# A two-layer decoder step on one core: another order in the routing with filler products, another order of the first layer's loads, and v in other PSUM banks

## The chip, the core and the metric

The kernel runs on one NeuronCore of a Trainium2 chip. The metric is the time of one execution on the device, in microseconds (us), as the median of several runs. The engines are TensorE (PE, with its weight loads shown as PEld), VectorE (DVE), ScalarE (ACT), GpSimd (POOL) and SyncE (SP), which issues nearly all transfers.

## What is computed

A decoder trunk of two layers over 288 tokens (32 of running sequences, 256 of a new one), 1024 features, all in float32:

```python
h = rmsnorm(x); z = h @ w_in                       # 1024 -> ua | ub | v, 512 each
# group A: diagonal complex state space model, 32 groups of 16 channels, 64 states
h_t = ab * h_(t-1) + bb @ ua_t ; ya = glu(gelu(Re(c @ h_t) + d * ua_t))
# group B: gated unit, 8 heads of 64, chunks of 128 positions
v = layernorm(gelu(v)) ; yb = gelu(ub) * (tril(w_s) @ v + b_s)
x = x + [rmsnorm(ya), rmsnorm(yb)] @ w_out
x = x + ffn(rmsnorm(x))     # layer 0: dense SwiGLU; layer 1: top 2 of 8 experts
```

Outputs are the final rmsnorm of x, the last states of both kinds of sequences, and the normalised v of the 32 running tokens.

## The kernel before

Every engine has one program, written out by hand in the order in which it works; they meet by semaphores (`wait_ge`, `then_inc`), and each engine takes its instructions strictly in order. Features lie on the 128 partitions, tokens on the free axis (KT = 8 blocks of x), so a 288-column product per weight block is the usual one. A float32 product shows as two records in the trace, each with a weight load. The expert and dense phases split each weight into a high part (ACT) and a low part (DVE, POOL) and use three products.

*Start and mixer (each layer).* SP loads cols, x, consts, misc, then `load_in`: B (`b_d`, lines 527 to 528, straight into the slots of BPX, in pieces of 32 numbers), w_in in four pieces (0 and 1 are the halves of ua's columns by feature block, 2 is v's, 3 is ub's), C, and small tables. PE waits for the constants (line 1035), sums the squares of x (`mean_sum`), forms ua with `u_half` in banks 0 to 3, then v in banks 0 to 2 (lines 1063 to 1068), then transposes the powers of B, four for each of n = 0 to 7, into banks n % 4 (lines 1071 to 1081), then the states' inputs (s, L1090), ub in banks 4 to 7 (L1098), the gates of the spatial unit (L1119 to L1128, four of them, ft = 0 to 3), with the kernel matrices K (L1112) ahead of ft = 2, then y (L1141, L1147), the GLU, and w_out (L1196, L1205).

ACT forms the roots, copies ua into `ust` (16 copies, L855), applies GELU to the three token tiles of v (`gelu_v`, L821), takes the deviations (`deviation`, L826), centres tiles 1 and 2 of v by eight instructions of 64 columns each (`centre`, L833), copies the transposed B (BT, L868) and s (L877), applies GELU to ub (L882), copies K (L886). In layer 0 ACT's first functions are exp and sin for the angles.

DVE (the helper at line 1412 holds every tensor_tensor) forms the angles, h of layer 0 by `gained`, the powers of B (BPX), scales ua, takes the statistics of v (`statistics`), forms the carried states (`carried`), normalises v (`layer_norm`), then does the states in two halves (rotate, scan L1654 and L1655, rotate back, `st_ready`), with the scaling of ub (`gate_rows`) between. layer_norm(2) stands behind the first scan, 0 and 1 before the states.

POOL forms the rotations (L663 to L678, layer 0 here, layer 1 in the dense phase), masks the spatial weights (L694), then the powers of C (CPX, L701 to L711, `cp_ready`), the diagonal, and adds it to K (L725, `k_ready`). PE waits for `cp_ready` at L1112 and for `k_ready` before y. SP loads w_out when the states are ready (`st_ready`, line 562), in the order of the feature blocks; its first half overlays B's powers and the state inputs.

*Routing (behind layer 1's w_out).* PE finishes transposes of the tokens (banks by `tok_bank`) and logits (`lg_mm`); DVE forms the two best experts of each token, `mask`, and the low parts of the tokens (L1785, six), PE the positions in each expert and the totals (L1269, L1271), DVE the one-hot tables (`one_hots`, L1795); ACT the high parts of the tokens (L945). PE gathers the tokens of two experts (`gather`, four times ten products of 256 columns, L1282 to L1285), ACT and DVE split them, and the first expert's gate products follow (L1294). SP waits for the number of passes (`ni_ready`) before it loads further expert weights.

## Time and profile before

| | us |
|---|---|
| median of 3 runs | 976.8 |
| lowest and highest | 972.62 and 979.61 |
| the profiled execution | 980.57 |
| its span, first to last instruction | 978.8 |
| mean granted clock of TensorE | 0.970 of full |

PE is busy for 930.1 us of the span, DVE for 713.5, ACT for 522.3, POOL for 321.7. An engine that is busy less than the span waits for others in the rest; only the engine that the end hangs on counts, and here PE is on 81% of the chain that ended last. A granted clock of 1.00 is 2.4 GHz, 0.50 is 1.2 GHz.

### The profile page before, as it was taken

The numbers are of one execution on the slowest core, as the hardware profiler recorded it, in microseconds if no ns is written. First come the engines' busy times: TensorE is split into PE (matmuls) and PEld (weight loads), VectorE is DVE, ScalarE is ACT, GpSimd is POOL, SyncE is SP. The second block draws the span as 40 slices with busy tenths as digits, with TensorE's granted clock in tenths as the row PEclk, the third lists the DMA queues.
The fourth block names the chain that finished last, engine by engine and source line by source line (L and its number), as shares of the span: only waits on it lengthen the run. The fifth ranks groups of instructions, "written<-read, shape, count | busy, mean of one in ns | idle before, by whom it ended". The sixth has DMA issues, their size and how long they took to land.

```text
span 978.8 us, 15158 instructions
## 1 busy us (share of the span) xinstructions
PE 930.1 (95%) x5526; PEld 789.7 (81%) x5526; DVE 713.5 (73%) x1032; ACT 522.3 (53%) x679; POOL 321.7 (33%) x260
## 2 busy tenths in 40 slices
PE   6999999998999999799998999999999999999895
PEld 4486779998999996386787888878888888878774
DVE  7799557574355508976375497988799988898784
ACT  3661445553333402661542567776777867685762
POOL 6996002212348100960020042231514051414220
PEclk9998999998999999987998999999999999999998
DMA  9500835554554118201800689897998989898861
GB/s 277 163 1 4 307 87 189 167 165 132 151 162 152 59 44 226 104 4 63 348 1 30 232 290 361 288 384 273 328 311 326 339 299 334 290 379 271 363 210 49
DMA packets 95564, 199.65 MB, mean 204 GB/s; under 512 B 34194, under 2 KB 55922, under 8 KB 95508
## 3 DMA queue, kind: packets, MB, share of 16 engines
q1 hardware_dynamic: 94708, 197.88, 59.1%
q8 instruction: 36, 0.59, 0.2%
q10 hardware_dynamic: 576, 0.59, 0.2%
q0 software_dynamic: 224, 0.43, 0.1%
q14 instruction: 20, 0.16, 0.0%
HBM read 197.27 MB, written 1.61 MB: 203 GB/s over the span
## 4 chain that ended last, share of the span: by engine, by line
PE 81%; DVE 10%; DMA 3%; issue 3%; ACT 2%; SPq 1%; DVEq 0%; ACTq 0%
PE ps L1295 8%; PE ps L1294 8%; PE ps L1297 8%; PE ps L1031 7%; PE ps L1032 7%; PE ps L1033 6%; PE ps L1205 5%; PE ps L1365 4%; PE ps L1366 4%; PE ps L1369 4%; PE ps L1044 2%; DVE M L1412 2%; PE ps L1098 2%; PE ps L1196 2%; PE ps L1026 1%
## 5 line engine op out<-in xcount | busy, mean ns | idle before, releaser
L1412 DVE TENSOR_TENSOR wrnd_u<-wraw_u,wrnd_u 128x1376 fp32r<-128x1376 f32 (+1 forms) x80 | 144.7, 1839 | 5.6 <-ACT wrnd_u L784 5.5
L784 ACT ACTIVATE wrnd_g<-wraw_g 128x1376 fp32r<-128x1376 f32 (+2 forms) x96 | 115.1, 1212 | 59.6 <-DMA wraw_g<-in_moe_w_down 36.5
L648 POOL TENSOR_TENSOR wrnd_g<-wraw_g,wrnd_g 128x1024 fp32r<-128x1024 f32 (+2 forms) x16 | 47.6, 2973 | 258.9 <-ACT wrnd_g L784 258.9
L1412 DVE TENSOR_TENSOR wrnd_g<-wraw_g,wrnd_g 128x1376 fp32r<-128x1376 f32 (+1 forms) x80 | 119.6, 1506 | 15.6 <-ACT wrnd_g L784 15.5
L784 ACT ACTIVATE wrnd_u<-wraw_u 128x1376 fp32r<-128x1376 f32 (+1 forms) x96 | 115.7, 1256 | 11.1 <-DMA wraw_u<-in_moe_w_gate 7.0
L648 POOL TENSOR_TENSOR wrnd_u<-wraw_u,wrnd_u 128x1376 fp32r<-128x1376 f32 (+1 forms) x16 | 52.4, 3275 | 80.8 <-ACT wrnd_u L784 80.8
L1031 PE MATMUL ps<-Md,split_u 128*128 128x288 f32 (+2 forms) x240 | 71.7, 299 | 5.4 <-DVE rs L1412 5.4
L1412 DVE TENSOR_TENSOR xb<-xb,ps 128x288 f32<-128x288 f32 x96 | 39.5, 445 | 50.2 <-PE ps L1205 25.6
L1033 PE MATMUL ps<-Md,split_u 128*128 128x288 f32 (+2 forms) x240 | 70.9, 296 | 0.0
L1031 PE MATMUL ps<-Md,split_d 128*128 128x288 f32 (+2 forms) x224 | 66.6, 297 | 0.8 <-DVE xb L1412 0.8
L1033 PE MATMUL ps<-Md,split_d 128*128 128x288 f32 (+2 forms) x224 | 66.2, 295 | 0.0
L1031 PEld LDWEIGHTS ps<-Md,split_u 128*128 128x128 f32 (+2 forms) x240 | 45.1, 188 | 5.9 <-DVE rs L1412 5.9
L1205 PE MATMUL ps<-D 128*128 128x288 f32 x192 | 49.3, 409 | 0.0
L1412 DVE TENSOR_TENSOR split_u<-raw,split_u 128x1024 fp32r<-128x1024 f32 (+2 forms) x22 | 29.3, 1332 | 27.3 <-ACT split_u L778 27.3
L1412 DVE TENSOR_TENSOR split_d<-raw,split_d 128x1024 fp32r<-128x1024 f32 (+2 forms) x21 | 29.7, 1424 | 26.5 <-ACT split_d L778 26.4
L640 POOL TENSOR_TENSOR split_u<-raw,split_u 128x1024 fp32r<-128x1024 f32 x8 | 19.9, 2482 | 82.6 <-ACT split_u L778 82.6
L640 POOL TENSOR_TENSOR split_d<-raw,split_d 128x1024 fp32r<-128x1024 f32 x7 | 17.1, 2444 | 89.1 <-ACT split_d L778 89.1
L1033 PEld LDWEIGHTS ps<-Md,split_u 128*128 128x128 f32 (+2 forms) x240 | 45.2, 189 | 0.0
L1032 PE MATMUL ps<-hbr,split_d 128*128 128x288 f32 (+1 forms) x152 | 45.2, 297 | 0.0
L1032 PE MATMUL ps<-hbr,split_u 128*128 128x288 f32 (+1 forms) x152 | 45.1, 297 | 0.0
L1205 PEld LDWEIGHTS ps<-D 128*128 128x128 f32 x192 | 36.0, 190 | 9.4
L1031 PEld LDWEIGHTS ps<-Md,split_d 128*128 128x128 f32 (+2 forms) x224 | 42.5, 190 | 1.0 <-DVE xb L1412 1.0
(355 smaller groups left out, 2662.0 us busy)
## 6 DMA issues: line engine op xcount, KB each, us to landing
wraw_u<-in_moe_w_gate SPq DMA_DIRECT2D x39, 688.0 KB, 6.5
wraw_g<-in_moe_w_up SPq DMA_DIRECT2D x32, 688.0 KB, 7.2
wraw_g<-in_moe_w_down SPq DMA_DIRECT2D x39, 512.0 KB, 4.5
wraw_u<-in_moe_w_down SPq DMA_DIRECT2D x33, 512.0 KB, 4.4
wraw_u<-in_moe_w_up SPq DMA_DIRECT2D x24, 688.0 KB, 6.1
wraw_g<-in_moe_w_gate SPq DMA_DIRECT2D x18, 688.0 KB, 5.7
raw<-in_ffn_w_gate SPq DMA_DIRECT2D x20, 512.0 KB, 4.5
raw<-in_ffn_w_up SPq DMA_DIRECT2D x20, 512.0 KB, 4.0
```

The costliest lines, as they stand in the source:

```text
L648: pool.tensor_tensor(lo[0:r, 0:w], raw_half(n)[0:r, 0:w], hi[0:r, 0:w].bitcast(F32), ALU.subtract).then_inc(w_lo_pool, 1)
L784: act.activation(halves(n)[0][0:r, 0:w], raw_half(n)[0:r, 0:w], ACT.Copy).then_inc(w_hi, 1)
L1031: pe.matmul(out, w_hi, x_hi, start=start, stop=False)
L1032: pe.matmul(out, w_hi, x_lo, start=False, stop=False)
L1033: return pe.matmul(out, w_lo, x_hi, start=False, stop=stop)
L1205: mm = pe.matmul(bank(out_bank[m]), w_out[:, k, m * P:(m + 1) * P], yn(k), start=(m >= 4 and k == 0), stop=(k == (MT - 1 if m < 4 else KT ...
L1294: pe.matmul(o, hg_h[hg][:, k, :], w_hi[:, f0:f1], start=(k == 0), stop=False)
L1295: pe.matmul(o, hg_h[hg][:, k, :], w_lo[:, f0:f1], start=False, stop=False)
L1297: mm = pe.matmul(ps[:, b0 + b, 0:f1 - f0], hg_l[hg][:, k, :], w_hi[:, f0:f1], start=False, stop=(k == KT - 1))
L1365: pe.matmul(ps[:, 6 + z, :], het_h[0:r, k, :], w_hi[0:r, f], start=(k == 0), stop=False)
L1366: pe.matmul(ps[:, 6 + z, :], het_h[0:r, k, :], w_lo[0:r, f], start=False, stop=False)
L1412: return dve.tensor_tensor(o, a, b, op)
```

## The change

- Routing: ACT and DVE take the token blocks in the order in which the gather reads them (TOK_ORDER), DVE forms three low parts before the one-hot tables and three behind; the first gather uses the banks 3, 5, 4, 6; the totals of the experts are formed between the second and third gather; 11 and 6 products of `ones` by `ones` into bank 0 stand ahead of the waits for the mask and for the tokens. The early `exp` on ACT that only loaded its table is gone. The first `lead_low` stands ahead of the gates' arithmetic.
- First layer: `ones` is written by DVE and not loaded; PE begins with 18 products of it; consts and misc are loaded behind w_in's second piece; B is loaded as one transfer with rows of 4 KB into a buffer of its own (`b_raw`, which overlays POOL's ct1 and ct2, so POOL waits for `b_used`); h of layer 0 is formed by ACT behind the squares.
- v goes to banks 4 to 6, so v doesn't wait for ua's banks, and the transposes of B wait for ua alone; the states' inputs wait for all of v's GELUs. One deviation for all three tiles stands behind the copies of BT; ACT centres all three tiles, 24 instructions, behind the copies of the states' inputs; DVE does all three layer norms behind its first scan.
- w_out: the second half is loaded as soon as all state inputs are multiplied, the first when the states are ready.

```diff
+TOK_ORDER = (2, 4, 0, 3, 5, 1)
+LEAD_BANK = (3, 5, 4, 6)
+FILL_MASK, FILL_TOK = 11, 6
...
+WARM_START = 18
...
+        b_raw = D[:, 5248:6272].rearrange("p (r n f) -> p r n f", r=2, n=NP)
...
-            sp.dma_start(consts[:, :], consts_d).then_inc(const_in, 16)
-            sp.dma_start(misc[:, :], misc_d).then_inc(const_in, 16)
...
-                for r in range(2):
-                    sp.dma_start(BPX[:, r, :, 0, :], b_d[l, :, r]).then_inc(prep_in, 16)
+                else:
+                    piece(0, 0, 4, 0)
+                sp.dma_start(b_raw, b_d[l]).then_inc(prep_in, 16)
+                piece(1, 4, KT, 0)
                 if l == 0:
-                    piece(0, 0, 4, 0)
-                piece(1, 4, KT, 0)
+                    sp.dma_start(consts[:, 0:4 * P], consts_d[:, 0:4 * P]).then_inc(const_in, 16)
+                    sp.dma_start(misc[:, :], misc_d).then_inc(const_in, 16)
...
-                for j in range(PIECES):
+                for j in (2, 3, 0, 1):
+                    if j == 0:
+                        sp.wait_ge(st_ready, 2 * (l + 1))
                     sp.dma_start(w_out[:, 2 * j:2 * j + 2, :], src[:, 2 * j:2 * j + 2, :]).then_inc(w_out_in[j], 16)
...
-                sp.wait_ge(st_ready, 2 * (l + 1))
+                sp.wait_ge(s_mm, 4 * (l + 1))
...
+                pool.wait_ge(b_used, l + 1)
...
-                    act.activation(v[0:n, t, :], ps[0:n, t, :], ACT.Gelu_apprx_tanh,
+                    act.activation(v[0:n, t, :], ps[0:n, 4 + t, :], ACT.Gelu_apprx_tanh,
                                    scale=r_tok[0:n, t:t + 1]).then_inc(v_ready, 1)
...
-                def deviation(g0, g1, n):
-                    act.wait_ge(var_ready, 2 * l + n)
-                    act.activation(std[:, g0:g1], stat[:, g0:g1, 1], ACT.Sqrt,
-                                   bias=eps[:, 0:1]).then_inc(std_ready, 1)
...
                 def centre(t):
-                    act.wait_ge(nmr_ready, 2 * l + t)
+                    n = TILES[t][1]
+                    act.wait_ge(nmr_ready, l + 1)
...
+                    for k in range(KT):
+                        act.activation(h[:, k, :], x[:, k, :], ACT.Copy, scale=col(0, "norm_mix", k)).then_inc(h_ready, 1)
...
-                deviation(0, 16, 1)
-                centre(1)
...
-                deviation(16, 24, 2)
+                act.wait_ge(var_ready, l + 1)
+                act.activation(std, stat[:, :, 1], ACT.Sqrt, bias=eps[:, 0:1]).then_inc(std_ready, 1)
...
-                centre(2)
+                for t in range(3):
+                    centre(t)
...
-            act.activation(warm, eps[:, 0:1], ACT.Exp)
...
-            for n in range(6):
+            for n in TOK_ORDER:
...
-            pe.wait_ge(const_in, 32)
+            pe.wait_ge(ones_ready, 1)
+            for n in range(WARM_START):
+                pe.matmul(bank(6, P), ones, ones, start=True, stop=True)
...
-                    pe.wait_ge(ua_ready, 4 * l + t + 1)
...
-                        mm = pe.matmul(ps[0:n, t, :], h[:, k, t0:t0 + n], w_in[:, k, 2 * MIX:IN_W],
+                        mm = pe.matmul(ps[0:n, 4 + t, :], h[:, k, t0:t0 + n], w_in[:, k, 2 * MIX:IN_W],
...
+                pe.wait_ge(const_in, 32)
...
-                    if n < 3:
-                        pe.wait_ge(v_ready, 3 * l + n + 1)
-                    elif n == 3:
-                        pe.wait_ge(ua_ready, 4 * l + 4)
+                    if n < 4:
+                        pe.wait_ge(ua_ready, 4 * l + n + 1)
...
+                pe.wait_ge(v_ready, 3 * (l + 1))
...
+            def fill(n):
+
+                for _ in range(n):
+                    pe.matmul(bank(0, P), ones, ones, start=True, stop=True)
+
+            fill(FILL_MASK)
             pe.wait_ge(mask_ready, 1)
...
-                    pe.matmul(ps[0:n, 7, 8 * t:8 * t + 8], lhs, mask[0:w, u, :], start=(u == 0), stop=(u == t))
-            for u, (_, w) in enumerate(TILES):
-                mm = pe.matmul(ps[:, 7, 24:32], ones[0:w, :], mask[0:w, u, :], start=(u == 0), stop=(u == 2))
+                    mm = pe.matmul(ps[0:n, 7, 8 * t:8 * t + 8], lhs, mask[0:w, u, :], start=(u == 0), stop=(u == t))
             mm.then_inc(pos_mm, 1)
-            pe.wait_ge(tokl_ready, 6)
+            fill(FILL_TOK)
+            pe.wait_ge(tokl_ready, 3)
             pe.wait_ge(tokz_ready, 1)
 
...
-                gather(r, 3 + r)
+                if r == 2:
+                    for u, (_, w) in enumerate(TILES):
+                        mm = pe.matmul(ps[:, 7, 24:32], ones[0:w, :], mask[0:w, u, :], start=(u == 0), stop=(u == 2))
+                    mm.then_inc(tot_mm, 1)
+                    pe.wait_ge(tokl_ready, 6)
+                gather(r, LEAD_BANK[r])
             for k in range(KT):
                 if k % 2 == 0:
...
-                    for k in range(KT):
-                        dve.wait_ge(x_in[k // 4], 16)
-                        gained(h[:, k, :], 0, "norm_mix", k)
...
-                dve.wait_ge(prep_in, 32 * (l + 1))
+                dve.wait_ge(prep_in, 16 * (l + 1))
...
-                    br, bi = BPX[:, 0, :, max(s - 1, 0), :], BPX[:, 1, :, max(s - 1, 0), :]
+                    br, bi = [BPX[:, r, :, s - 1, :] if s else b_raw[:, r] for r in range(2)]
...
+                    o_r = tt(o_r, o_r, bt1, ALU.subtract)
+                    if s == 0:
+                        o_r.then_inc(b_used, 1)
...
                 def layer_norm(t):
 
-                    n, g = TILES[t][1], slice(8 * t, 8 * t + 8)
-                    vt = v[0:n, t, :].rearrange("p (h d) -> p h d", h=NH)
-                    if t:
-                        dve.wait_ge(vc_ready, 2 * l + t)
-                    else:
-                        link(tt(vt, vt, bc(stat[0:n, g, 0], HD), ALU.subtract))
-                        link(tt(vt, vt, bc(std[0:n, g], HD), ALU.mult))
+                    n = TILES[t][1]
+                    dve.wait_ge(vc_ready, 3 * l + t + 1)
                     link(tt(v[0:n, t, :], v[0:n, t, :], lng[0:n, :], ALU.mult))
                     tt(v[0:n, t, :], v[0:n, t, :], lnb[0:n, :], ALU.add).then_inc(vn_ready, 1)
...
                 link(statistics(0))
-                statistics(1).then_inc(var_ready, 1)
+                link(statistics(1))
+                statistics(2).then_inc(var_ready, 1)
                 if l:
                     carried()
-                dve.wait_ge(std_ready, 2 * l + 1)
-                link(dve.reciprocal(std[:, 0:16], std[:, 0:16]))
-                dve.scalar_tensor_tensor(nmr[:, NH:2 * NH], stat[:, NH:2 * NH, 0], -1.0, std[:, NH:2 * NH],
-                                         ALU.mult, ALU.mult).then_inc(nmr_ready, 1)
-                layer_norm(0)
-                statistics(2).then_inc(var_ready, 1)
-                layer_norm(1)
-                dve.wait_ge(std_ready, 2 * l + 2)
-                link(dve.reciprocal(std[:, 16:24], std[:, 16:24]))
-                dve.scalar_tensor_tensor(nmr[:, 2 * NH:3 * NH], stat[:, 2 * NH:3 * NH, 0], -1.0, std[:, 2 * NH:3 * NH],
-                                         ALU.mult, ALU.mult).then_inc(nmr_ready, 1)
-
+                dve.wait_ge(std_ready, l + 1)
+                link(dve.reciprocal(std, std))
+                dve.scalar_tensor_tensor(nmr, stat[:, :, 0], -1.0, std, ALU.mult, ALU.mult).then_inc(nmr_ready, 1)
...
-                        layer_norm(2)
+                        for t in range(3):
+                            layer_norm(t)
...
-            for n in range(6):
+            def token_low(i):
+
+                n = TOK_ORDER[i]
...
-                dve.wait_ge(tokh_ready, n + 1)
+                dve.wait_ge(tokh_ready, i + 1)
...
+
+            for i in range(3):
+                token_low(i)
             dve.wait_ge(pos_mm, 1)
...
+            def lead_low(r):
+
+                both = ps[:, LEAD_BANK[r], :].rearrange("p (k s) -> p k s", s=2 * P)
+                k = slice(2 * r, 2 * r + 2)
+                dve.wait_ge(hgh_ready, r + 1)
+                tt(hg_l[0][:, k, :], both[:, :, 0:P], hg_h[0][:, k, :].bitcast(F32), ALU.subtract).then_inc(hgl_ready, 1)
+                return tt(hg_l[1][:, k, :], both[:, :, P:2 * P], hg_h[1][:, k, :].bitcast(F32), ALU.subtract)
+
             one_hots(0)
+            for i in range(3, 6):
+                token_low(i)
+            lead_low(0)
...
+            dve.wait_ge(tot_mm, 1)
...
-            for r in range(4):
...
-                last = tt(hg_l[1][:, k, :], both[:, :, P:2 * P], hg_h[1][:, k, :].bitcast(F32), ALU.subtract)
+            for r in range(1, 4):
+                last = lead_low(r)
             last.then_inc(hgbl_ready, 1)
```

## Rows read from the trace of the kernel before

**Rows 1.** The page: busy time, share and instructions of each engine.

```profile
PE 930.1 (95%) x5526; PEld 789.7 (81%) x5526; DVE 713.5 (73%) x1032; ACT 522.3 (53%) x679; POOL 321.7 (33%) x260
```

**Rows 2.** PE timeline, layer 0: start, us, line, operation, count [idle before <-releaser].

```profile
7.97 5.84 PE L1026 MATMUL ps<-M,consts 128*128 128x288 f32 x16 [7.97 <-DMA misc<-in_misc]
14.12 15.76 PE L1044 MATMUL ps<-hb,G 128*128 128x288 f32 x64 [0.31 <-DMA G<-in_w_in]
...
62.70 15.73 PE L1098 MATMUL ps<-hb,G 128*128 128x288 f32 x64
...
84.25 2.02 PE L1112 MATMUL ps<-U,D 128*32 128x128 f32 x64 [0.70 <-POOL U L711]
...
92.41 2.70 PE L1141 MATMUL ps<-M 128*128 128x288 f32 x8
...
112.54 3.15 PE L1196 MATMUL ps<-D 128*128 128x288 f32 x12 [0.37 <-DMA D<-in_w_out]
```

**Rows 3.** PE timeline, layer 1, v to ub.

```profile
409.74 1.04 PE L1080 MATMUL ps<-consts,D 128*128 128x128 f32 x8
418.06 4.26 PE L1080 MATMUL ps<-consts,D 128*128 128x128 f32 x24 [7.28 <-ACT M L821]
...
429.26 15.73 PE L1098 MATMUL ps<-hb,G 128*128 128x288 f32 x64
```

**Rows 4.** Windows: busy us (count) of PE, PEld, DVE, ACT, POOL; PEclk; DMA; GB/s.

```profile
92.40:105.00 12.60, 12.60 (x289) 11.03 (x287) 9.46 (x20) 2.56 (x7) 1.14 (x2) 0.83 0.46 170
...
410.00:418.00 8.00, 0.78 (x8) 0.54 (x5) 7.83 (x8) 4.72 (x11) 7.84 (x7) 0.76 0.00 0
...
530.00:536.00 6.00, 4.20 (x18) 3.96 (x18) 5.83 (x17) 2.61 (x6) 0.00 (x0) 0.52 0.00 1
```

**Rows 5.** POOL timeline, powers of C in both layers.

```profile
50.97 1.49 POOL L708 TENSOR_TENSOR U<-D,U 128x512 f32<-128x512 f32 x1
...
59.39 1.04 POOL L708 TENSOR_TENSOR U<-D,U 128x512 f32<-128x512 f32 x1
...
82.49 1.71 POOL L711 TENSOR_TENSOR U<-U,D 128x512 f32<-128x512 f32 x1
...
426.77 1.29 POOL L711 TENSOR_TENSOR U<-U,D 128x512 f32<-128x512 f32 x1
```

**Rows 6.** DVE timeline, layer 0, first half of the states; 74.01 is layer_norm(2).

```profile
60.11 1.40 DVE L1412 TENSOR_TENSOR fin<-fin,D 128x64 f32<-128x64 f32 x2 [0.67 <-ACT D L877]
...
69.88 0.46 DVE L1412 TENSOR_TENSOR M<-ps,rs 128x288 f32<-128x288 f32 x1
...
74.01 3.03 DVE L1412 TENSOR_TENSOR M<-M,D 128x512 f32<-128x512 f32 x2
```

**Rows 7.** DVE timeline, layer 1; 436.20 is layer_norm(2).

```profile
426.70 1.44 DVE L1412 TENSOR_TENSOR fin<-fin,D 128x64 f32<-128x64 f32 x2 [1.21 <-ACT D L877]
...
436.20 1.42 DVE L1412 TENSOR_TENSOR M<-M,D 128x512 f32<-128x512 f32 x2
```

**Rows 8.** ACT timeline: squares of x in layer 0, centre(1) in layer 1.

```profile
6.44 2.76 ACT L765 ACTIVATE M<-xb 128x288 f32<-128x288 f32 x8
...
413.25 2.76 ACT L833 ACTIVATE M<-M,U 128x64 f32<-128x64 f32 x8 [6.50 <-DVE U L1615]
```

**Rows 9.** PE timeline, routing: positions, gather, first expert.

```profile
530.05 2.73 PE L1269 MATMUL ps<-G,consts 32*32 32x8 f32 x12 [2.77 <-DVE G L1412]
...
536.12 0.55 PE L1282 MATMUL ps<-Me 128*128 128x256 f32 x1 [1.88 <-DVE Me L1795]
...
540.52 0.28 PE L1282 MATMUL ps<-Me 128*128 128x256 f32 x1
...
542.91 0.39 PE L1294 MATMUL ps<-wrnd_g,hbr 128*128 128x512 f32 x1
```

**Rows 10.** ACT and DVE timelines, routing.

```profile
527.60 1.28 ACT L939 ACT_TABLE_LOAD   x1
...
530.24 4.16 DVE L1785 SCALAR_TENSOR_TENSOR Me<-ps,G,Me 32x512 fp32r<-32x512 f32 x6
```

More of the change, by code:

```diff
@@ L354, in build @@
         const_in = sem("const_in")
+        ones_ready = sem("ones_ready")
+        b_used = sem("b_used")
         prep_in = sem("prep_in")
@@ L448, in build @@
         pos_mm = sem("pos_mm")
+        tot_mm = sem("tot_mm")
         ni_ready = sem("ni_ready")
@@ L820, in gelu_v @@
                     act.wait_ge(rt_ready, 3 * l + t + 1)
-                    act.activation(v[0:n, t, :], ps[0:n, t, :], ACT.Gelu_apprx_tanh,
+                    act.activation(v[0:n, t, :], ps[0:n, 4 + t, :], ACT.Gelu_apprx_tanh,
                                    scale=r_tok[0:n, t:t + 1]).then_inc(v_ready, 1)
-                def deviation(g0, g1, n):
-                    act.wait_ge(var_ready, 2 * l + n)
-                    act.activation(std[:, g0:g1], stat[:, g0:g1, 1], ACT.Sqrt,
-                                   bias=eps[:, 0:1]).then_inc(std_ready, 1)
                 def centre(t):
-                    act.wait_ge(nmr_ready, 2 * l + t)
+                    n = TILES[t][1]
+                    act.wait_ge(nmr_ready, l + 1)
                     for g in range(NH):
-                        vh, at = v[:, t, g * HD:(g + 1) * HD], t * NH + g
-                        vc = act.activation(vh, vh, ACT.Identity, bias=nmr[:, at:at + 1], scale=std[:, at:at + 1])
+                        vh, at = v[0:n, t, g * HD:(g + 1) * HD], t * NH + g
+                        vc = act.activation(vh, vh, ACT.Identity, bias=nmr[0:n, at:at + 1], scale=std[0:n, at:at + 1])
                     vc.then_inc(vc_ready, 1)
@@ L954, in _ @@
                 act.wait_ge(gather_mm, r + 1)
-                both = ps[:, 3 + r, :].rearrange("p (k s) -> p k s", s=2 * P)
+                both = ps[:, LEAD_BANK[r], :].rearrange("p (k s) -> p k s", s=2 * P)
                 act.activation(hg_h[0][:, 2 * r:2 * r + 2, :], both[:, :, 0:P], ACT.Copy)
@@ L1519, in angle_dve @@
                     link(tt(q(28), q(28), q(24), ALU.mult))
+            dve.memset(ones, 1.0).then_inc(ones_ready, 1)
             link(dve.memset(eps[:, :], EPS))
@@ L1546, in _ @@
                     link(tt(o_i, fr, bi, ALU.mult))
-                    tt(o_r, o_r, bt1, ALU.subtract)
+                    o_r = tt(o_r, o_r, bt1, ALU.subtract)
+                    if s == 0:
+                        o_r.then_inc(b_used, 1)
                     last = tt(o_i, o_i, bt2, ALU.add)
@@ L1817, in add_scattered @@
                 add_to_x(k, (END_BANK if end else SCATTER_BANK)[k])
+            def lead_low(r):
+                both = ps[:, LEAD_BANK[r], :].rearrange("p (k s) -> p k s", s=2 * P)
+                k = slice(2 * r, 2 * r + 2)
+                dve.wait_ge(hgh_ready, r + 1)
+                tt(hg_l[0][:, k, :], both[:, :, 0:P], hg_h[0][:, k, :].bitcast(F32), ALU.subtract).then_inc(hgl_ready, 1)
+                return tt(hg_l[1][:, k, :], both[:, :, P:2 * P], hg_h[1][:, k, :].bitcast(F32), ALU.subtract)
             one_hots(0)
+            for i in range(3, 6):
+                token_low(i)
+            lead_low(0)
             for r in range(1, MAXPASS):
@@ L1836, in _ @@
             dve.tensor_scalar(ni_sb[:, :], cn[:, 1:2], 3.0, None, ALU.add).then_inc(ni_ready, 1)
-            for r in range(4):
-                both = ps[:, 3 + r, :].rearrange("p (k s) -> p k s", s=2 * P)
-                k = slice(2 * r, 2 * r + 2)
-                dve.wait_ge(hgh_ready, r + 1)
-                tt(hg_l[0][:, k, :], both[:, :, 0:P], hg_h[0][:, k, :].bitcast(F32), ALU.subtract).then_inc(hgl_ready, 1)
-                last = tt(hg_l[1][:, k, :], both[:, :, P:2 * P], hg_h[1][:, k, :].bitcast(F32), ALU.subtract)
+            for r in range(1, 4):
+                last = lead_low(r)
             last.then_inc(hgbl_ready, 1)
```

## The prediction

> **What bounds the kernel now.** I read the page first, then the engine timelines of three stretches that the change touches, then the waits and the granted clock there. TensorE (PE) is busy 95% of the span [rows 1], so only two things can move the time: its idle gaps and the stretches in which its clock is low. The gaps lie outside the two big matrix phases, in the places that the change edits. At the start PE begins at 7.97 us, when the last constant has landed, and after the first mean it goes on at 14.12 us, when the first quarter of w_in has [rows 2]. In layer 0 it then runs almost without a gap until 0.70 us before L1112, where it waits for POOL's powers of C; 0.37 us more go for w_out [rows 2]. In layer 1 it stands for 7.28 us between two transposes, waiting for ACT's GELU of v, and the transposes after it take 4.26 us [rows 3]. In the routing it stands 2.77 and 1.88 us, and the gather then runs from 536.12 to 542.91 [rows 9].
>
> **Layer 1: the 7.28 us gap.** Before, v lies in banks 0 to 2, which the transposes of B reuse, so transpose n=2 waits for the third GELU of v. That GELU stands on ACT behind centre(1), eight instructions in 2.76 us, and these waited 6.50 us for DVE's scale [rows 8], which stood behind carried(). After the change v has banks 4 to 6, and before its third GELU ACT has nothing but copies. v ends at 409.74; all 32 transposes at the speed of the first ones (8 in 1.04 us, overlapping, so 32 in 3.8 to 4 [rows 3]) end near 413.6 instead of 422.3. ACT's third GELU (0.7) and the first copy of BT (0.6) end near 411.1, early enough for transpose n=4. The eight copies end near 415, 1.5 us behind the transposes, then come a table load (1.28, as on ACT in rows 10) and a root (0.3) before the first copy of the states' inputs, at 417.3; this holds the third group of state matmuls by 0.2 to 0.5. ub, begun at 429.26 [rows 3], then begins near 420.9: gain 8.4 us. So much is it if nothing later binds.
>
> What can bind is DVE, since all three layer norms now stand between its first scan and the spatial gate. Statistics of tile 2 end near 412.3, carried() follows (5.9 us before, beside POOL), scale and first state work begin near 419.2 instead of 426.70 [rows 7]. The rotation before the scan took 9.7 us beside a busy POOL in layer 0 (60.11 to 69.8 [rows 6]); POOL's powers of C end at 428.05 [rows 5], so I take the slow value: 428.9, gate rows 0.4 and two scans 2.4 at free speed: 431.7. One layer norm (two products with 512 columns) took 1.42 us free [rows 7] and 3.03 us beside POOL [rows 6]; three free ones make 4.3: 436.0. PE ends ub at 420.9 + 15.73 = 436.6 [rows 3]. No wait, by 0.6 us. ACT's 24 centring instructions (8.3 us [rows 8]) run from 421.6 to 429.9 and are in time. The bounds: 8.4 us, and 4.8 less if the three norms take 9.1 us.
>
> The Trainium skill (GPSIMD Engine Reference, Specifications) says that GpSimd shares its SBUF interfaces with VectorE and that the two collide when VectorE reads two SBUF inputs. These rows agree, 1.42 against 3.03 us for the same pair; by that rule alone each norm moved in front of POOL's end would cost double, and layer 1 would gain 3.6 instead of 8.4.
>
> **Layer 0: the start.** PE no longer waits for constants: ones are written by DVE. 18 warming products of 128 columns run from about 1 us; at the slow rate seen at the start (16 records of 288 columns in 5.84 us [rows 2]) they end near 7 to 8 us, when the first squares are there (6.44 + 0.43 [rows 8]). The first mean, 16 records of 0.24 us, ends near 11. The gains of h are now eight ACT copies behind the squares, 9.2 to 12.0, which delays nothing, as ACT's root had waited for PE. The first quarter of w_in is issued at 2.1 instead of 7.64 us, no longer behind two transfers of B in rows of 128 bytes, and lands about 9 to 10. So u begins near 10.8 instead of 14.12 [rows 2]: 3.3 us earlier, and so does all PE work down to ub, which would end at 74.8 instead of 78.4.
>
> This gain meets a wall. L1112 is released by POOL, whose chain of rotations and powers of C ends at 82.49 + 1.71 = 84.2 [rows 5] and starts from the angles of DVE, which the change leaves. Nothing of the change takes work from POOL. DVE runs fewer two-input products beside it: the two that centred tile 0 go and some 2 us move behind, and POOL's step costs 1.49 against 1.04 us beside a busy or an idle DVE [rows 5]: about 4 x 0.3 = 1.2 us, so 83.0 to 84.2. The state work on DVE starts 3.8 us earlier, at 56.3, reaches the norms at 70.1 and, with three at 2.9 to 3.03 [rows 6], leaves them at 78.9 instead of 77.04. So PE stands from 74.8 to about 79.0, does two of four gates (5.1 us) until 84.1, and is where it was. Then DVE's last gate rows come at 86.3 to 87.7 instead of 85.9, ACT's last GELU and its four copies of K (2.43) and POOL's sum (1.26) follow, and y begins at 91.2 to 92.4 instead of 92.41 [rows 2]. The second half of the states is ready near 98.6 to 99.7; y needs it 7.3 us after its own start, at 98.5 to 99.7, so it comes just in time. Without an effect of the clock layer 0 gives 0 to 1.2, and 0.37 for w_out, whose half needed first no longer waits for the states: up to 1.6 us.
>
> **The clock in layer 0.** The new standstill of 4.2 us is where nothing stood before. The granted clock was 0.52 on average in 530 to 536, after 2.8 us of idleness, and it fell to half within the 7.28 us of layer 1 (0.76 over 410 to 418) [rows 4]. I expect the fall to half, 1.2 GHz, here too. Then two gates of 2.56 take up to 4.2 each, and the 64 short products of K 3.6 instead of 2.0: y up to 3.8 later; against that the original had its own slow stretch there (0.83 in 92.4 to 105 [rows 4]), worth 1.8. Net loss 0.3 to 1.5 us. I take 0.5 us of loss for layer 0.
>
> **Routing.** Before: mask at 530.0, six low parts of tokens on DVE at 0.68 = 4.16 us to 534.4, positions and one-hots to 536.0, gather at 536.12 [rows 9, 10]. After: only three low parts stand ahead (2.04 us): 532.3; the copies on ACT begin at 527.9, as the early table load of exp (1.28 [rows 10]) is gone, so they are ahead, and the load comes behind them, when ACT has time; the six count products stand behind the second of the four gathers. PE's 12 position products, 2.73 us at the low clock [rows 9], are done by 531.5 with the filling, which itself (11 and 6 products, 22 and 12 records of 0.11 us) fits into the gaps: 527.3 to 529.8 and 531.5 to 532.8. Positions and one-hots take 1.66 again: gather at 534.0, 2.1 us earlier. It took 40 products in 6.79 us, the first 20 at 0.213, the rest at 0.12 [rows 9]; at 0.12 throughout 4.8: 2.0 saved. The counts put into it, six records of 0.11, cost 0.7. The other three low parts end at 536.0, before gather 2 needs them (537.1). First lead_low at 536.8; the others at 540.1 to 541.5, needed at 543.2. Sum 2.1 + 2.0 - 0.7 = 3.4 us. If the filling does not keep the clock the 2.0 are lost and the 12 products take 1.4 longer, partly hidden: 1.4 left.
>
> The expert phase behind follows PE: its loads are released by used slots, so the gain is carried.
>
> **Sum.** Layer 1 8.4, routing 3.4, layer 0 -0.5: 11.3 us. The profiled execution took 980.57 us (span 978.8 and 1.8 around it), so 969.3; the median of the three runs is 976.8, 3.8 less, so 965.5 for the median. The runs before lie between 972.62 and 979.61, and part of that is where the low stretches of the clock fall.
>
> **The rivals.**
> *A, the start survives.* If POOL is faster than I hold, or PE's clock is kept, layer 0 gives 1.6 to 3.7 instead of -0.5. For it: POOL's spans are rough and a third shorter beside an idle DVE. Against it: its chain has over 70 us and one bound. 963.4 to 961.3.
> *B, the norms bind in layer 1.* They still run beside POOL: 9.1 instead of 4.3, PE stands 4.2 us there, and its clock falls again as in layer 0 (1 to 3 us). For it: POOL ends only 3 us before the norms begin, and DVE's early start keeps it busier. 965.5 + 4.2 + 2 = 971.7.
> *C, other side: the norms become the release of both gates.* If the state work of layer 0 doesn't start earlier (ACT's copies of u and its GELUs set it), the norms end at 78.9 + 3.8 = 82.7 and the two gates at 87.8, 3.7 behind POOL; with the clock's 2 to 3 more layer 0 gives -6. In layer 1 the norms then end 6 us behind ub, and with the clock the 8.4 are gone. Left are the routing's 3.4: 976.8 + 6 - 3.4 = 979.4. It decides from the point where the norms end more than 6 us behind ub in layer 1.
> *D, the filling does nothing for the clock.* For it: 12 short products stood at half clock between two gaps [rows 4, 9]. Against it: it leaves gaps of 0.3 and 1.2 us only. 965.5 + 2.0 to 3.0 = 967.5 to 968.5.
>
> **Chances.** Forecast (963 to 968.5) 0.47, A 0.17, B 0.17, C 0.05, D 0.14. Eight in ten: 959.5 to 973, from A's lower part to B with the spread of the runs. A measurement of this kernel tells about 1% from no change, that is 9.8 us: under 967.0 counts as faster. Forecast mostly and A: 0.6; B, D and the forecast's upper edge within: 0.37; C with the clock: 0.03.
>
> **What the profile would show.** Layer 1: no wait between the transposes of B, ub at 421. Layer 0: u at 10.8, a new wait of some 4 us before the first gate on a DVE norm, L1112 still released by POOL near 84, a low clock around 79 to 90. Routing: gather 7 us after the last logits, its 40 products at 0.12 us, low parts not awaited. Wrong would be: a wait for vn in layer 1, L1112 well before 83, a gather with clock 0.5.

## The result, and the profile after

| | median of the runs | profiled execution | its span, clock |
|---|---|---|---|
| before | 976.9 us (972.6 to 979.6, 4 runs) | 980.57 us | 978.8 us, 0.970 |
| after | 967.5 us (964.2 to 967.8, 4 runs) | 964.18 us | 962.4 us, 0.985 |

The change makes the kernel 0.9% faster: ratio 0.9909, 95% interval 0.9884 to 0.9934, 9.4 us. A second measurement of the same kernel gave 0.9886 (0.9851 to 0.9920). The predicted 965.5 us is 2 us off. The two profiled executions lie 16.4 us apart, 7 more than the medians; the milestones below show where these 7 are.

I follow PE through four points. The first is where u of layer 1 goes on after its short wait for DVE (0.6 to 0.7 us). Length of each stretch in the profiled executions:

| stretch of PE | before | after | change | predicted |
|---|---|---|---|---|
| start to u of layer 1 (second half) | 370.10 | 377.17 | +7.07 | +0.5 |
| u to the GLU products, layer 1 | 106.58 | 93.04 | -13.54 | -8.4 |
| GLU products to the end of the logits | 50.60 | 50.60 | 0.00 | 0 |
| logits to the first expert product | 15.63 | 12.82 | -2.81 | -3.4 |
| expert phase to the end | 435.89 | 428.77 | -7.12 | 0 |

Up to the first expert product the gain is 9.3 us, close to the medians' difference of 9.4. That they agree so well is chance, since the second row alone spreads from 91.1 to 97.6 us over the kernels with the new order of v. Nothing ties the last row to the change: it spreads from 428.8 to 436.3 us over the 14 profiles of this study, with the same products there, though with one profile of the kernel before this isn't shown.

So the sum was nearly right, and two of its terms were not: layer 0 lost 7 us where 0.5 was expected, and layer 1 gained 5 more than expected. That the two cancel is luck.

**Layer 1 and routing.** PE's timeline of the kernel after (start, us, line, shape, count, idle before and releaser), to be read against [rows 3]:

```profile
416.81 3.66 PE L1090 MATMUL ps<-consts,D 128*128 128x128 f32 x32
...
427.58 15.73 PE L1109 MATMUL ps<-hb,G 128*128 128x288 f32 x64
...
448.36 2.02 PE L1123 MATMUL ps<-U,D 128*32 128x128 f32 x64
...
470.21 4.04 PE L1171 MATMUL ps<-M,D 128*128 128x288 f32 x16
```

The 32 transposes are one row; the 7.28 us between the eighth and the ninth are gone. The products of K take 2.02 us; in the kernel before they took 3.66, at a low clock:

```profile
451.57 3.66 PE L1112 MATMUL ps<-U,D 128*32 128x128 f32 x64
```

And in the routing, against [rows 9]:

```profile
520.67 2.70 PE L1278 MATMUL ps<-consts 128*128 128x128 f32 x22
523.58 1.71 PE L1286 MATMUL ps<-G,consts 32*32 32x8 f32 x12 [0.21 <-DVE G L1433]
...
527.81 0.35 PE L1298 MATMUL ps<-Me 128*128 128x256 f32 x1 [1.08 <-DVE Me L1809]
...
530.37 0.93 PE L1339 MATMUL ps<-G,consts 32*128 32x8 f32 x6
...
533.63 0.39 PE L1310 MATMUL ps<-wrnd_g,hbr 128*128 128x512 f32 x1
```

The x22 row is the first part of the filling. The 12 position products take 1.71 instead of 2.73 us, and the gather, now with the counts inside it, 5.8 instead of 6.8.

**Layer 0**, against [rows 2]:

```profile
11.03 15.68 PE L1056 MATMUL ps<-hb,G 128*128 128x288 f32 x64
...
58.91 15.73 PE L1109 MATMUL ps<-hb,G 128*128 128x288 f32 x64
80.64 0.66 PE L1130 MATMUL ps<-M,consts 1*128 1x64 f32 x2 [6.00 <-DVE M L1433]
...
90.33 3.29 PE L1123 MATMUL ps<-U,D 128*32 128x128 f32 x64
...
98.58 1.52 PE L1152 MATMUL ps<-M 128*128 128x288 f32 x8
...
106.46 1.07 PE L1158 MATMUL ps<-M,U 128*32 128x72 f32 x51 [0.56 <-issue]
...
113.27 1.81 PE L1036 MATMUL ps<-hb,consts 128*128 128x288 f32 x4 [1.86 <-issue]
114.88 5.09 PE L1171 MATMUL ps<-M,D 128*128 128x288 f32 x16
```

u and ub are 3.1 and 3.8 us earlier. Then PE stands 6.00 us for the norms on DVE and is 6.2 us late at y. The windows of the same stretch (busy us and count of PE, PEld, DVE, ACT, POOL; PEclk; DMA share; GB/s):

```profile
80.60:90.00 9.40, 9.36 (x20) 5.05 (x20) 9.19 (x17) 1.33 (x3) 5.69 (x6) 0.50 0.04 9
90.00:98.00 8.00, 8.00 (x83) 5.44 (x83) 7.79 (x10) 2.35 (x4) 1.69 (x1) 0.81 0.00 0
...
110.00:120.00 10.00, 8.13 (x41) 5.94 (x30) 4.28 (x7) 4.48 (x6) 0.00 (x0) 0.83 0.96 336
```

After the standstill the granted clock is 0.50, the lower of the two levels (1.2 GHz): the first two gates take 9.7 us instead of 5.1, K 3.3 instead of 2.0.

DVE (the norms of layer 0 and of layer 1), against [rows 6, 7], and POOL against [rows 5]:

```profile
71.32 9.06 DVE L1433 TENSOR_TENSOR M<-M,D 32x512 f32<-32x512 f32 x6
...
437.91 4.10 DVE L1433 TENSOR_TENSOR M<-M,D 32x512 f32<-32x512 f32 x6
```

```profile
79.80 1.71 POOL L724 TENSOR_TENSOR U<-U,D 128x512 f32<-128x512 f32 x1
...
96.31 1.77 POOL L738 TENSOR_TENSOR M<-M,D 128x512 f32<-128x512 f32 x1 [9.99 <-ACT M L897]
```

The six products of the norms take 9.06 us beside POOL's products of C and 4.10 in layer 1, where POOL had finished C at 433.3. POOL itself is through with C at 81.5 instead of 84.2: it is no longer what PE waits for.

### The profile page after: what moved, and what is told of

It reads as the page before. It is cut to its first block, busy times and chain, and to the rows that moved or that the text cites. A ratio compares the mean times of both kernels' runs of the same rounds, so it can differ in the third digit from the quotient of the medians.

```text
span 962.4 us, 15298 instructions
## 1 busy us (share of the span) xinstructions
PE 927.3 (96%) x5596; PEld 788.0 (82%) x5596; DVE 702.4 (73%) x1017; ACT 525.0 (55%) x696; POOL 326.9 (34%) x260
## 4 chain that ended last, share of the span: by engine, by line
PE 90%; DVE 6%; issue 2%; ACT 1%; DMA 0%; DVEq 0%; ACTq 0%
PE ps L1311 8%; PE ps L1310 8%; PE ps L1313 8%; PE ps L1041 7%; PE ps L1042 7%; PE ps L1043 7%; PE ps L1216 5%; PE ps L1077 4%; PE ps L1386 4%; PE ps L1387 4%; PE ps L1390 4%; PE ps L1056 3%; PE ps L1036 2%; PE ps L1207 2%; PE ps L1109 2%
## 5 line engine op out<-in xcount | busy, mean ns | idle before, releaser
L1433 DVE TENSOR_TENSOR wrnd_g<-wraw_g,wrnd_g 128x1376 fp32r<-128x1376 f32 (+1 forms) x80 | 129.0, 1625 | 14.5 <-ACT wrnd_g L797 14.4
L1433 DVE TENSOR_TENSOR wrnd_u<-wraw_u,wrnd_u 128x1376 fp32r<-128x1376 f32 (+1 forms) x80 | 131.5, 1678 | 5.3 <-ACT wrnd_u L797 5.3
L660 POOL TENSOR_TENSOR wrnd_u<-wraw_u,wrnd_u 128x1376 fp32r<-128x1376 f32 (+1 forms) x16 | 57.2, 3577 | 77.5 <-ACT wrnd_u L797 77.5
L1041 PE MATMUL ps<-Md,split_u 128*128 128x288 f32 (+2 forms) x240 | 71.3, 297 | 5.4 <-DVE rs L1433 5.4
```

What stands on the lines that cost most here:

```text
L660: pool.tensor_tensor(lo[0:r, 0:w], raw_half(n)[0:r, 0:w], hi[0:r, 0:w].bitcast(F32), ALU.subtract).then_inc(w_lo_pool, 1)
L1041: pe.matmul(out, w_hi, x_hi, start=start, stop=False)
L1433: return dve.tensor_tensor(o, a, b, op)
```

## The experiments

Ratios are to the kernel before on the same chip. Medians of one kernel taken twice differ by up to 3 us, so the timelines carry more of the argument than the last column.

| kernel | median us | before, same chip | ratio (95%) |
|---|---|---|---|
| filling in layer 0's standstill | 958.7 | 976.2 | 0.9857 (0.9801 to 0.9914) |
| the same again, more runs | 961.3 | 975.1 | 0.9863 (0.9836 to 0.9890) |
| norms ahead | 961.5 | 976.2 | 0.9858 (0.9816 to 0.9899) |
| norms ahead in layer 0, filling 8 and 7 | 958.9 | 974.8 | 0.9807 (0.9767 to 0.9846) |
| norms ahead in layer 0, filling 4 and 4 | 958.5 | 975.1 | 0.9841 (0.9813 to 0.9868) |
| after, again | 964.4 | 974.8 | 0.9886 (0.9851 to 0.9920) |
| after, v in banks 0 to 2 | 968.3 | 974.8 | 0.9917 (0.9887 to 0.9947) |
| after, constants and warming undone | 971.5 | 976.2 | 0.9948 (0.9921 to 0.9975) |
| after, no filling in the routing | 969.1 | 976.2 | 0.9941 (0.9916 to 0.9967) |
| before + v and centring alone | 970.5 | 975.1 | 0.9959 (0.9938 to 0.9980) |
| before + routing alone | 973.1 | 975.1 | 0.9989 (0.9964 to 1.0014) |

**1. Is it the standstill's clock that costs layer 0 its time?** The wait stays as long, but PE multiplies ones through it:

```diff
+                pe.wait_ge(s_ready, 4 * (l + 1))
+                for _ in range(FILL_NORM[l]):      # (22, 0)
+                    pe.matmul(bank(2, P), ones, ones, start=True, stop=True)
                 pe.wait_ge(vn_ready, 3 * (l + 1))
-                pe.wait_ge(s_ready, 4 * (l + 1))
```

> The kernel after, with 22 extra products of ones (128 columns, into a bank that nobody reads; 0.245 us each in the routing of the kernel after, so 5.4 us) put in front of the wait for the layer norms in layer 0 alone. Theory S (standstill and clock): the 6.0 us of standstill from 74.6 to 80.6 make the clock fall to 0.50, and two gates and the products of K then take 13.0 us instead of 5.1 + 2.0; kept busy, the gates begin at the same 80.6, at clock 1.00, K starts near 85.8, y near 93 instead of 98.6: 962 for the median, 5 to 6 us faster than the kernel after. Theory P (POOL or DVE sets the start of y, the clock does not matter): y at 96 to 98.6, 966 to 967.5, no difference. Theory T (the stalls behind y, 0.56 and 1.86 us, and the clock of 0.80 to 0.85 from 110 to 120 come from the transfers and not from the late y): y comes 5 us earlier but the stalls stay or grow, 963.5 to 965.

PE's timeline of this kernel:

```profile
75.47 5.07 PE L1118 MATMUL ps<-consts 128*128 128x128 f32 x44
80.47 0.43 PE L1133 MATMUL ps<-M,consts 1*128 1x64 f32 x2
...
85.59 2.02 PE L1126 MATMUL ps<-U,D 128*32 128x128 f32 x64
...
92.57 1.53 PE L1155 MATMUL ps<-M 128*128 128x288 f32 x8
...
105.36 4.04 PE L1174 MATMUL ps<-M,D 128*128 128x288 f32 x16
```

and its windows:

```profile
80.60:90.00 9.40, 9.40 (x94) 5.88 (x94) 9.19 (x17) 3.60 (x7) 5.59 (x6) 1.00 0.04 9
90.00:98.00 8.00, 8.00 (x156) 6.31 (x156) 7.79 (x11) 0.49 (x2) 1.27 (x1) 1.00 0.68 240
```

The gates begin when they did (80.5 against 80.6), DVE is as busy (9.19) and POOL nearly (5.59 for 5.69), and what differs on PE is the clock: 1.00 for 0.50. y is 6.0 us earlier, the GLU 9.5, u of layer 1 10.3 (366.83). Theory S holds in this place; theory P, by which the clock would not matter, falls, and so does theory T for this execution, as PE has no stall behind y. By the medians it is 5.8 to 8.8 us faster than the kernel after (964.4 and 967.5); the ratio is 0.3 to 0.5% lower by its middle, and the intervals overlap. The repeat:

> The kernel after with 22 filling products in layer 0's standstill, as in the first run of this kind, beside the run before this one on one chip. 958.7 again, 0.982 of the kernel before; theory S: clock 1.00 from 74.6 to 92, y at 92 to 93, no wait on a norm. If the first run was luck: 963 to 966.

The repeat had no standstill either (0.23 us), y at 93.11, GLU at 107.72 and u of layer 1 at 369.20. The clock fell once with no wait in front of it, from the last gate into y (0.57 in 91.6 to 95), and there was one stall of 0.44 us. Its 961.3 us lie between the two expectations. So the order of events in the timeline is shown twice; the gain in the median is 3 to 9 us by pairs of medians, and no better known than that.

**2. Shorten the wait instead.** On DVE the norms go between the two halves of the rotation:

```diff
                     link(tt(wr, wr, tmp, ALU.add))
+                    if q == 0:
+                        for t in range(3):
+                            layer_norm(t)
+                        gate_rows(0)
                     tt(v8(wi), si, cr, ALU.mult)
...
                     link(dve.tensor_tensor_scan(wi, mg, wi, 0.0, ALU.mult, ALU.add))
-                    if q == 0:
-                        for t in range(3):
-                            layer_norm(t)
-                        gate_rows(1)
```

> The kernel after, with the three layer norms and the first gate row moved, on DVE, ahead of the second half of the rotation (behind wr), so ahead of the scans, in both layers; nothing else. DVE's total is the same. Theory S: the norms then end near 71.5 (centred tiles are there at 62.4, 65.1, 67.7), before PE ends ub at 74.6; PE does two gates from 74.6 to 79.7 at clock 1.00 and stands before K until POOL's powers of C, 81.5 to 84.2; y near 91.5 instead of 98.6: 961 for the median, 5 to 7 us faster than the kernel after, if the second half of the states (97 to 98.5 on DVE, needed 7.3 us behind the start of y) does not bind. Theory P: POOL is slowed beside the busier DVE and K comes at 84.2 or later; the clock falls in that gap as well, y at 95 to 96: 964 to 965. In layer 1 neither expects a change (norms had 1.2 us to spare).

PE, in the kernel with the norms ahead:

```profile
81.81 2.02 PE L1123 MATMUL ps<-U,D 128*32 128x128 f32 x64 [2.03 <-POOL U L724]
...
90.66 2.86 PE L1152 MATMUL ps<-M 128*128 128x288 f32 x8 [1.70 <-POOL M L738]
```

The norms end at 70.5, the gates start at once behind ub, and the order of waits is what theory S said: now POOL binds twice, 2.03 and 1.70 us. y is 7.9 us earlier, u of layer 1 8.7 (368.47). In its profile 4.6 us were lost again in layer 1, where the clock fell under the gates and K with no wait in front (0.82 in 430 to 443, 0.66 in 443 to 456). It was not tried whether that belongs to the order or to this execution. The kernel of experiment 7 shows the same kind of fall in the same stretch (0.74 in 443 to 456), without this order.

**3. Both together**, in layer 0 alone, with filling in front of K and of y.

> The kernel after, in layer 0 alone with the norms ahead of the second half of the rotation (as in the earlier run) and 8 filling products in front of the products of K and 7 in front of y, where PE stood 2.03 and 1.70 us. Theory S: clock 1.00 throughout, K at 81.8 to 82.2, y at 90.7 to 91, w_out at 107.3 (109.2 with the filling alone, 111.1 with the norms ahead alone, 119.8 in the kernel after): 957 for the median, 1 to 2 us faster than the filling alone. If only the standstill's length counts and not the clock: as with the norms ahead alone, 961.5.

```profile
78.55 1.73 PE L1138 MATMUL ps<-M,consts 1*128 1x512 f32 x2
80.21 2.07 PE L1142 MATMUL ps<-D,M 128*128 128x256 f32 x4
82.08 3.62 PE L1121 MATMUL ps<-consts 128*128 128x128 f32 x16
85.63 2.02 PE L1126 MATMUL ps<-U,D 128*32 128x128 f32 x64
...
94.17 1.53 PE L1157 MATMUL ps<-M 128*128 128x288 f32 x8
```

Neither theory's y. The clock fell at 78.6, in the second gate, although PE had not stood still since its start, and the filling, now at half clock, took 3.62 us, all of it behind the time at which POOL's C is ready (81.6 in this kernel): K was held back by 3.5. So less filling:

> The kernel after with the norms ahead of the second half of the rotation in layer 0, and half as many filling products as before in front of K and of y (4 and 4, 1.0 us each). If the filling that was too long at a low clock (3.62 us in front of K, 1.6 past the release) was what kept the sum of both from being better than the filling alone: K at 81.8 to 83.5, y at 91 to 92, w_out at 107.5 to 109, 956 to 957. If the falls of the clock in this stretch come with the short products themselves whatever stands between them: 958 to 960, like either alone.

```profile
79.93 1.05 PE L1121 MATMUL ps<-consts 128*128 128x128 f32 x8
81.41 2.02 PE L1126 MATMUL ps<-U,D 128*32 128x128 f32 x64 [0.43 <-POOL U L725]
...
90.78 1.84 PE L1157 MATMUL ps<-M 128*128 128x288 f32 x8
...
97.81 1.63 PE L1157 MATMUL ps<-M 128*128 128x288 f32 x8 [1.33 <-DVE M L1438]
```

K and y come 0.2 to 0.4 us before the range of the first expectation. But w_out begins at 109.16, and the median of 958.5 us lies in the range of the second (958 to 960), so these runs don't tell the two apart. The wait has moved once more, to the second half of the states (1.33 us), the fourth thing in a row that binds. With a ratio of 0.9841 this beats the kernel before, and by 6 to 9 us of the medians the kernel after, whose second measurement's interval it overlaps; between it and the filling alone the runs don't decide.

**4. The kernel after, again.**

> The kernel after, unchanged, so that it shares its chip and its runs of the kernel before with the three that follow. 967.5 as before, ratio 0.991; its profile shows how much the 6 us of standstill and what follows differ from run to run (y at 98.6 in the first profile). Theory S: the standstill and the low clock behind it are in every execution, y between 96 and 100. If they are chance (the first profile was an odd one), y comes near 93 here.

Standstill 4.90 us, gates at 80.53, clock 0.50 in 80.6 to 90, y at 98.32. In the five profiles that share this stretch (this one, the first, and those of experiments 6 to 8) y begins at 98.1 to 100.5. It was no odd execution.

**5. The start undone**, as far as the constants and the warming products go. B's single transfer and h on ACT stay.

> The kernel after, with the start undone: the constants are loaded right behind x, PE waits for them, and the 18 warming products are gone. So u begins near 13 to 14 instead of 11.0. Theory S: all work up to ub is 2 to 3 us later, but the norms on DVE begin later by as much, so the standstill stays at 6 us and y comes 2 to 3 us later: 969.5 to 970.5. Theory W (wall, as predicted: POOL and DVE's chain set the time at which the gates go on, and an earlier start is given back): y at 98.6 all the same, standstill 3 to 4 us and less low clock: 966 to 968, no difference.

```profile
14.42 15.68 PE L1056 MATMUL ps<-hb,G 128*128 128x288 f32 x64
...
82.35 0.65 PE L1130 MATMUL ps<-M,consts 1*128 1x64 f32 x2 [4.31 <-DVE M L1433]
...
102.20 2.70 PE L1152 MATMUL ps<-M 128*128 128x288 f32 x8
```

u is 3.4 us later, the gates 1.7, y 3.6 (part of it a second fall of the clock at 99), the median 4 to 7 and the ratio 0.4 to 0.6% worse. Against the other profiles with the new start, u (11.0 to 12.0 there) is 2.4 to 3.4 later and the gates (80.5 to 80.7 there) 1.7 to 1.8. So the early start is given back in part, in a standstill of 4.31 us for 4.9 to 6.0, and not all of it. How much the kernel keeps in the end the clock's falls hide.

**6. The routing without the filling**, FILL_MASK and FILL_TOK 0:

> The kernel after, without the 17 filling products in the routing. If the filling keeps the clock (forecast): PE stands 2.7 and 1.6 us more, the clock falls to near 0.5, the 40 products of the gather take 6.8 instead of 4.8 and the positions 2.7 instead of 1.7: 2 to 3 us slower, 969.5 to 970.5. If the filling does nothing for the clock (rival D): 967.5, no difference.

```profile
524.60 2.79 PE L1286 MATMUL ps<-G,consts 32*32 32x8 f32 x12 [2.77 <-DVE G L1433]
529.25 0.55 PE L1298 MATMUL ps<-Me 128*128 128x256 f32 x1 [1.86 <-DVE Me L1809]
```

Both standstills of [rows 9] and the half clock are back; logits to first expert take 14.60 us instead of 12.82. With the filling the new routing took 12.8 to 13.5 us over eleven profiles, so the filling is worth 1.1 to 1.8 us there, and rival D falls.

**7. Is it v's banks, or the place of centre?** v returns to banks 0 to 2 and the transposes wait for v_ready, as before.

> The kernel after with v in banks 0 to 2 again, so that transpose n = 0 to 2 of B wait for the GELU of v as in the kernel before; ACT centres all tiles behind the states as in the kernel after. Theory C (the gap of 7.28 us in layer 1 came from centre(1), which waited for DVE, ahead of the third GELU): there is a wait of only 0.7 to 1.3 us in each layer for the last GELU; 1 to 2 us slower than the kernel after, 968.5 to 969.5. Theory B (the banks are what makes the gain): the gap comes back with several us in layer 1, with a low clock behind it: 973 to 976.

```profile
413.49 4.88 PE L1078 MATMUL ps<-G,hb 128*128 128x512 f32 x11
418.21 3.78 PE L1093 MATMUL ps<-consts,D 128*128 128x128 f32 x32
```

No gap in layer 1 (nor in layer 0): the 32 transposes take 3.78 instead of 3.66 us. Theory C was right in kind and too high in size (0.1 for 0.7 to 1.3). The other banks add nothing to speak of; the gap goes by not having eight centring instructions, which wait for DVE, ahead of the third GELU on ACT. The median is 3.9 us above the kernel after's on the same chip, and its profile 6.9. Of these 2.4 lie in layer 0, with a clock of 0.76 in 98 to 110, and 4.4 in layer 1, where the two gates, K and the other two gates took 16.3 us for 12.1:

```profile
450.94 3.66 PE L1126 MATMUL ps<-U,D 128*32 128x128 f32 x64
```

The edit changes nothing in either place. So the slow K of the kernel before comes back here in full, with no gap ahead of it.

**8. The stalls without a waiting semaphore.** The loads of the dense weights wait for glu_mm:

> The kernel after, with the loads of layer 0's dense weights held back until PE has done the GLU products (near 120 us), so that only w_out is on the DMA engines from 98 to 109 and nothing from 110 to 120. Theory T (the stalls that PE has without a waiting semaphore, 0.56 us at 106.5 and 1.86 at 113.3, are PE's own instructions fetched behind the weight transfers): the stall at 113.3 is gone and the one at 106.5 stays, since w_out is still on its way; GLU begins at 113.0 instead of 114.9; 1.5 to 2 us gained there. Theory O (something else): both stalls stay, GLU at 114.9. The dense phase begins 30 us later than the held loads, which may or may not be covered.

```profile
112.19 1.13 PE L1037 MATMUL ps<-hb,consts 128*128 128x288 f32 x4 [1.04 <-issue]
```

One execution, 963.1 us. The stalls are 0.76 us at 106.20 and 1.04 at 112.19 (0.40 and 1.59 at 106.04 and 112.59 in the kernel after, again). Theory T falls for the second stall, which stays although the dense loads are gone and w_out has landed: the DMA share is 0.02 in 110.5 to 112.2 and 0.00 from 111 to 117. It needs no transfer beside it. The first falls while w_out is on its way, but in the first kernel of experiment 1 w_out was on its way as well and PE had no stall. The cause of both stays open; they cost 0 to 4.8 us in an execution.

**9. Two parts alone.**

> The kernel before with only the second part of the change: v in banks 4 to 6, ACT centring all three tiles behind the states, one root for all tiles, the three norms behind DVE's first scan. Start, routing and the order of w_out are the old ones. Theory S: layer 0 loses with this part alone, as the norms end near 82.3 while PE ends ub at 78.4: standstill 3.9 us, clock 0.5, y near 100 to 102 instead of 92.4 and the dense phase 7 to 9 us later than 147.8; layer 1 gains 8.8 from the gap and up to 4.3 by the clock. Sum -5 to +2 us of gain against the kernel before, best guess 2 to 4 faster: 973 to 975. If the part does in layer 0 only what was predicted (0.5 us of loss): 968.

```profile
82.50 0.40 PE L1114 MATMUL ps<-M,consts 1*128 1x64 f32 x2 [4.75 <-DVE M L1407]
...
99.41 1.53 PE L1136 MATMUL ps<-M 128*128 128x288 f32 x8
...
413.65 3.66 PE L1074 MATMUL ps<-consts,D 128*128 128x128 f32 x32
```

The v part brings the standstill of layer 0 by itself, with y 7.0 us later than before; u of layer 1 is 3.9 late (374.00), then layer 1 takes 93.7 instead of 106.6. The median, 970.5, lies between the two expectations; the standstill, its length and the late y are theory S's.

> The kernel before with only the routing part of the change: order of the tokens' low parts, three of them behind the one-hots, count products behind the second gather, no early load of exp, banks of the gather, 17 filling products. As forecast: from the end of the logits to the first expert product 3.4 us less (13.0 to 13.6 instead of 16.4), everything before it unchanged: 973 to 974 for the median, ratio 0.9965. If the gain of the routing in the kernel after is owed to the other parts (the clock there), nothing: 976 to 977.

```profile
526.32 4.25 PE L1271 MATMUL ps<-consts 128*128 128x128 f32 x22
530.50 1.71 PE L1279 MATMUL ps<-G,consts 32*32 32x8 f32 x12
...
534.07 0.35 PE L1291 MATMUL ps<-Me 128*128 128x256 f32 x1 [0.42 <-DVE Me L1814]
```

Logits to first expert 13.43, 2.2 us less than before. (The 16.4 of the expectation counts from 0.8 us earlier than the table's 15.63 does, so its 13.0 to 13.6 stand for 12.2 to 12.8 here, and were missed.) The filling began at the low clock, 4.25 us for 2.70, and at its end the clock was full again. The measured ratio can't tell this from nothing.

## Why the prediction came out right, and where it was wrong

- *Layer 1, the gap:* right. Transposes without a wait, ub 1.7 us earlier in a layer that began 7.1 later, so 8.8 for the predicted 8.4. The norms end at 441.93, ub at 443.2: 1.3 us to spare (0.6 predicted), so rival B did not come. The reason given was right too (centre(1) on ACT), but the sum credited the pair "other banks and centring"; experiment 7 gives it to the centring alone.
- *Layer 1, the clock:* missing term, of unknown cause. The two gates, K and the other two gates took 16.76 us before and 12.5 after: 4.3 of the 5.1 us that layer 1 gained beyond the forecast. The low clock right behind the gap was in the sum, as the slow transposes (4.26 us). This second fall comes at 448, after 30 us of work without a wait, and the prediction has no term for it. Whether it belongs to the gap is not shown. Both profiles with the gap have it (16.8 and 16.6 us); of the twelve without it, nine took 12.1 to 12.6, and experiments 1, 2 and 7 have one of 13.7, 16.4 and 16.3. So layer 1 is 9.0 to 15.4 us shorter in the kernels that have the v part, and the part of it above 9 may come or not.
- *Layer 0, the standstill:* seen, with its place and its cause, and priced too low. The three norms took 9.06 us for 8.8, but DVE reached them at 71.3 instead of 70.1, and with the gate row PE stood 6.0 for 4.2. The gates took 9.7 for "up to 4.2 each", K 3.3 for 3.6. The bad step is the price of the clock behind that, and its netting. The start of y without the clock, 91.2 to 92.4, was nearly right: it was 92.6 and 93.1 with the filling. The "up to 3.8" for the clock was too low, 5.2 to 6.0 by experiment 1 and its repeat. Then 1.8 us were taken off for an old slow stretch. That did go, but stalls without a semaphore (2.4 us) and a clock of 0.83 in 110 to 120 took more than it gave. At u of layer 1 the kernel after is 7.0 to 10.3 us behind the two kernels with filling, where the 0.5 of the forecast counted 2 net for the clock. Experiment 1 shows the clock as the mechanism: the same wait without the fall.
- *The wall at POOL:* wrong. Its last product of C ended at 81.5, 1.5 us before the lowest value allowed (83.0), as rival A said. The prediction took 1.2 us off POOL's chain for fewer products of DVE beside it; in the kernel with the v part alone, with the old start, C ended at 80.9 for 84.2, 3.3 us. K did not wait for POOL at all and began at 90.33, behind the slow gates. A's 1.6 to 3.7 us did not come, as DVE was later than POOL by then. But A named a second way, "or PE's clock is kept", and with the filling layer 0 gained 3.3 and 0.9 us. The start is not lost either, experiment 5.
- *w_out:* the 0.37 us wait is gone. But SP still stood at k_ready, which came with the late K, and issued w_out at 98.2 (98.0 before): nothing of it was loaded earlier.
- *Routing:* 2.8 of 3.4. The gather starts 7.0 us behind the logits, as said, and 1.1 to 1.8 of the gain hang on the filling, as experiment 6 shows.
- *Rival C* did not come, since layer 1 had slack; in layer 0 alone it is nearly what happened (-6 there, -7 measured), from a start that did come earlier.

The sum of 11.3 us (9.3 measured) thus holds two errors of 6.6 and 5.1 us against each other, and that it came out is luck. Both are errors in the price of the clock: in layer 0 the fall behind the new standstill was priced too low, in layer 1 a fall that the kernel before had and the kernel after did not was not priced at all. The first is shown by experiment; the cause of the second is open.

The Trainium skill (TensorE: Matmul & The Clock Gate, HAM oscillation) says that a wait between stretches of work, if it is long enough, returns the engine to its low clock. The 6.00 us of standstill with 0.50 behind it agree. What the Trainium skill (GPSIMD Engine Reference, Specifications) says of VectorE's products with two inputs beside GpSimd agrees once more with the norms: 3.02 us each beside POOL, 1.37 without.

## What to carry to other kernels

An idle gap on the bounding engine has two prices, its length and the clock behind it, and a change that brings a gap must be charged with both; in layer 0 the second (5.2 to 6.0 us at y) was as large as the first (6.0). Filling a wait that can't be shortened with products that nobody reads is cheap, if it ends before the release even when PE comes late and at half clock; in experiment 3 it did not, and cost 3.5 us. When several waits lie close behind each other (DVE, POOL, POOL, DVE here, each within some 2 us), removing one is worth only the distance to the next. And a sum that comes out right is no proof of its terms: here only the milestones of the timeline showed the two errors.

## What the hardware showed unexpectedly

- The clock also fell with no idle time just before it: at 78.6 in experiment 3, under the gates and K of layer 1 in the kernel before (0.74 in 443 to 456), in experiment 2 (0.66) and in experiment 7 (0.74), with PE busy throughout. It didn't in the kernel after, again (K in 2.03 us at clock 1.00). These stretches have products of 64 to 512 columns, most with one row or 32 as contraction; what in them matters was not tried.
- PE stalled 0.2 to 2.5 us in y or the mean behind it with nothing to wait for that the profile shows, in nearly every profile, and once with no transfer running (experiment 8); the most in one execution was 4.8 us (experiment 6).
- The expert phase, with the same products in all 14 profiles, took 428.8 to 436.3 us, and 432.2 and 436.3 in two profiles of one kernel (experiment 1). One profile against one profile can't show a change of 1% here; the stretches between milestones can.
